# One matmul per group written as two of 128 columns, in a two-block network on one core

## The reference, cut to what matters

```
proj = rmsnorm(h) @ w_in + b_in
h = h + merged @ w_out
h = h + (silu(gate) * val) @ w_down        # gate, val from rmsnorm(h) @ w_up
...
proj = rmsnorm(h) @ w_in_2
h = h + merged @ w_out_2
h = h + square(relu(rmsnorm(h) @ mlp_w1)) @ mlp_w2
```

## Time and profile before

| | |
|---|---|
| median of three runs | 2766.68 us |
| the profiled execution's own time | 2776.59 us |
| its span, first to last instruction | 2774.7 us |
| TensorE busy | 2727.6 us (98%), 22990 matmuls |
| VectorE busy | 1702.0 us (61%) |
| ScalarE busy | 1294.1 us (47%) |
| mean granted TensorE clock | 0.993 of full |
| bytes moved by DMA | 503.31 MB, mean 181 GB/s |

### The profile page before, as it was taken

The page is one execution under the profiler, slowest core; times in us unless marked ns, Lnnn a source line. Parts: engine busy times, 40 slices in busy tenths (PEclk is TensorE's granted clock), DMA queues, the critical chain, the costliest instruction groups (busy, mean ns, idle before and its releaser), DMA issues.

```text
span 2774.7 us, 53033 instructions
## 1 busy us (share of the span) xinstructions
PE 2727.6 (98%) x22990; PEld 2710.7 (98%) x22990; DVE 1702.0 (61%) x1727; ACT 1294.1 (47%) x1458; POOL 1.8 (0%) x14
## 2 busy tenths in 40 slices
PE   7999999999999999999989999999999999999998
PEld 6999999999999999999989999999999999999998
DVE  4555564566667567646785687676665455554555
ACT  4444544444545345434553466664444343343443
POOL 0000000000000000000000000000000000000000
PEclk9999999999999999999999999999999999999999
DMA  5446555555555555555545555555555555555652
GB/s 190 142 148 197 193 186 184 190 187 183 181 188 190 189 194 188 193 191 171 171 149 182 169 181 182 183 197 193 189 189 189 182 182 195 183 184 187 191 183 107
DMA packets 257822, 503.31 MB, mean 181 GB/s; under 512 B 10150, under 2 KB 19038, under 8 KB 257630
## 3 DMA queue, kind: packets, MB, share of 16 engines
q1 hardware_dynamic: 255348, 500.50, 54.7%
q10 hardware_dynamic: 2298, 0.26, 0.1%
HBM read 498.63 MB, written 2.10 MB: 180 GB/s over the span
## 4 chain that ended last, share of the span: by engine, by line
PE 93%; DVE 4%; ACT 2%; issue 1%; ACTq 0%; DVEq 0%
PE psum L547 28%; PE psum L548 28%; PE psum L549 28%; PE psum L574 2%; PE psum L575 2%; PE psum L576 2%; DVE wlo L1289 1%; ACT whi L864 1%; DVE work L1317 0%; DVE hn L1327 0%; ACT hn L885 0%; DVE work L1614 0%; ACTq L853 0%; PE psum L787 0%; PE psum L789 0%
## 5 line engine op out<-in xcount | busy, mean ns | idle before, releaser
L1289 DVE TENSOR_TENSOR wlo<-raw,whi 128x1024 fp32r<-128x1024 f32 x952 | 1160.3, 1223 | 977.0 <-ACT whi L864 974.8
L864 ACT ACTIVATE whi<-raw 128x1024 fp32r<-128x1024 f32 x952 | 1003.6, 1058 | 1299.1 <-PE psum L549 1186.6
L547 PE MATMUL psum<-hn,whi 128*128 128x256 f32 x4448 | 1248.9, 281 | 10.8 <-DVE wlo L1289 10.6
L548 PE MATMUL psum<-hn,whi 128*128 128x256 f32 x4448 | 1246.0, 280 | 0.0
L549 PE MATMUL psum<-hn,wlo 128*128 128x256 f32 x4448 | 1245.9, 280 | 0.0
L547 PEld LDWEIGHTS psum<-hn,whi 128*128 128x128 f32 x4448 | 845.9, 190 | 15.1 <-issue 12.9
L549 PEld LDWEIGHTS psum<-hn,wlo 128*128 128x128 f32 x4448 | 842.9, 190 | 0.0
L548 PEld LDWEIGHTS psum<-hn,whi 128*128 128x128 f32 x4448 | 841.2, 189 | 0.1
L547 PE MATMUL psum<-act,whi 128*128 128x256 f32 x2544 | 714.1, 281 | 13.8 <-DVE wlo L1289 9.7
L549 PE MATMUL psum<-act,wlo 128*128 128x256 f32 x2544 | 713.5, 280 | 0.0
L548 PE MATMUL psum<-act,whi 128*128 128x256 f32 x2544 | 713.4, 280 | 0.0
(11 more groups left out here) (220 smaller groups left out, 949.9 us busy)
## 6 DMA issues: line engine op xcount, KB each, us to landing
raw<-in_w_in SPq DMA_DIRECT2D x160, 1024.0 KB, 5.1
raw<-in_mlp_w SPq DMA_DIRECT2D x128, 1024.0 KB, 5.2
raw<-in_w_up SPq DMA_DIRECT2D x80, 1024.0 KB, 5.0
raw<-in_w_down SPq DMA_DIRECT2D x40, 1024.0 KB, 5.1
raw<-in_w_out SPq DMA_DIRECT2D x32, 1024.0 KB, 5.1
raw<-in_w_branch_m SPq DMA_DIRECT2D x8, 1024.0 KB, 5.0
raw<-in_w_branch_c SPq DMA_DIRECT2D x8, 1024.0 KB, 5.1
raw<-in_w_up SPq DMA_DIRECT2D x8, 768.0 KB, 4.4
```

Of the source, the lines that this page charges most:

```text
L547: mm(o, hi[:, kk, w], both[:, 0, :], start=first and m % 2 == 0, stop=False)
L548: mm(o, hi[:, kk, w], both[:, 1, :], start=False, stop=False)
L864: A(whi[:, n % SLOTS, :], raw[:, n // 2 % RAW, n % 2 * HALF:(n % 2 + 1) * HALF], ACT.Copy)\
L1289: V.tensor_tensor(wlo[:, n % SLOTS, :], raw[:, n // 2 % RAW, n % 2 * HALF:(n % 2 + 1) * HALF], whi[:, n % SLOTS, :].bitcast(F32), ALU.subt ...
```

## The change

In the second half of every group, for the first row tile and the first output tile, the product of the high weights with the high activations is issued as two matmuls with the same weights, one over token columns 0 to 127 and one over 128 to 255. Neither has a start flag; the old one had none there either. The rest of the program is as it was.

```diff
                         for m in range(tiles):
                             o = psum[:, 4 * s + m // 2, m % 2 * T:(m % 2 + 1) * T]
                             w = slice(m * P, (m + 1) * P)
-                            mm(o, hi[:, kk, w], both[:, 0, :], start=first and m % 2 == 0, stop=False)
+                            if k == 1 and kk == 0 and m == 0:
+
+                                mm(o[:, 0:P], hi[:, kk, w], both[:, 0, 0:P], start=False, stop=False)
+                                mm(o[:, P:T], hi[:, kk, w], both[:, 0, P:T], start=False, stop=False)
+                            else:
+                                mm(o, hi[:, kk, w], both[:, 0, :], start=first and m % 2 == 0, stop=False)
                             mm(o, hi[:, kk, w], both[:, 1, :], start=False, stop=False)
```

## The result

The changed kernel takes **2730.07 us**, the median of four runs (2727.45 to 2732.62), against 2766.28 us for the kernel before. The ratio is 0.9862, with a 95% interval of 0.9816 to 0.9907. It is 36 us faster, where 12.8 us slower was forecast. The profiled execution's own time went from 2776.59 to 2727.69 us.

A forecast was written before the change was run, and what follows sets the result against it. TensorE, busy 98% of the span, was taken to bound the kernel. Of 118 pairs, five were given away: (118 - 4 - 1) x 0.1133 = +12.8 us on 2766.68 gives 2779.5 us, range 2774.5 to 2792.

The forecast's parts named there:

- the unit of everything below: Pace of 256-column float32r matmuls on TensorE, read from 1999.93 to 2003.67 us: 0.1133 us each, used to price every pair.
- The other groups keep 0.1133 us: Expected sign in the changed profile: matmuls outside the pairs go on stepping at 0.1133 us.
- 118 pairs: Count of groups going through `group`, each getting one pair, so TensorE should have 118 matmuls more.
- +0.113 us a pair, bound by the weight load: Each narrow matmul takes 0.113 us for its weight load, so a pair costs 0.226 against 0.113.
- The single distances of 0.113 us: Expected sign in a steady stretch: narrow matmul, second narrow one and following wide one start 0.113 us apart each.
- No less than nothing: Low end kept for a pair's cost: 0, if only moving columns counted; high end +0.327 us, or +0.414.
- `down_2` keeps its length: TensorE idled 13.1 us in 64 us there, so its four pairs were put at nothing; 0.45 us if uncovered.
- The cheap pair: Rival: narrow weight loads are fast or overlapped, so +0 to +2.9 us in all, 2766.7 to 2769.6; chance 0.09.
- the switch: Rival: the narrow pair also costs one step of 0.087 us, 23.6 us in all, about 2790; chance 0.05.
- the full-precision pace: Rival: a 128-column float32r matmul takes 0.22 us, 38.6 to 48.9 us in all, 2805 to 2816; chance 0.10.
- The 16-column transposes' 0.069 us: Step read for the 16-column transposes, 1.10 / 16, taken as evidence of a faster kind of weight load.
- The Trainium skill's rule: Page's sustained 81 ns per 128-column matmul with load: +49 ns a pair, +5.8 us in all; isolated formula +0.3 us.

## Why the prediction was wrong

The step that failed is in the first part: "33 steps, 3.74 / 33 = 0.1133 us each", and "That is the unit of everything below". It was true of 4 us at 2000 us and was carried to the whole program, down to the last part, where "The other groups keep 0.1133 us". Two thirds of the matmuls ran at 117.8 ns, and no rival had a place for it.

By the steps of the forecast:

- *118 pairs*: right.
- *+0.113 us a pair, bound by the weight load*: right. 352 more pairs cost 0.113 us each, and the loads start 0.11 us apart across a pair.
- *The single distances of 0.113 us*: wrong in form. They are 0.06, 0.11 and 0.17, three times 0.113 in sum. The second narrow matmul starts 0.06 us behind the start of its own load (707.31 and 707.25), where the others stand 0.11 behind theirs.
- *No less than nothing*: wrong, and not by a mis-sized term but by a missing one. The sum with it: (13989 - 543) long matmuls fewer, 4.5 ns each, is -60.5 us; the pairs are 118 x 0.127 = +15.0 us; together -45.5 us. The profiled execution lost 48.9 us. The other 3 us I did not trace. Laid side by side by instruction, 1200 matmuls took 4.6 us less where the kernel before was in the long rhythm (from 2180 us on), and 0.5 to 1.0 us more where both were in the short one (887 to 1160 us): the pairs alone.
- *`down_2` keeps its length*: right. The 64 us of the earlier trace rows took 63.8 us before and 63.6 us after, from the start of one instruction to that of the same other.
- *The cheap pair, the switch, the full-precision pace*: none took place. A step like the switch's does stand behind each pair (0.17), but it is part of the 0.127. The switch's price of 0.087 us was misread to begin with: in the earlier trace rows the first float32r matmul is followed late, after 0.20 us, but it also starts early, 0.14 us behind the two records that otherwise take 0.22. Together that is 0.34 us, and 0.22 + 0.12 without a seam: nearly nothing.
- *The 16-column transposes' 0.069 us*: it has the last one's latency in it. Their starts are 0.062 us apart; no term of the sum hangs on it.
- *The Trainium skill's rule*, "TensorE: Matmul & The Clock Gate", section "Back-to-back issue gap", with 81 ns for 128 columns and their loads: the runs speak against it for narrow float32r matmuls that stand between wide ones, at 0.113 us for a further pair in place of a wide matmul, so 113 ns for each narrow one; a sustained stream of 128-column float32r matmuls, which is what the page speaks of, no run has. The estimate by that page's formula for the isolated matmul, +0.3 us in all, fits still less.

Why -36 us in the medians and -49 in the profiles: the kernel before was profiled in one of its longer executions. In the experiments its runs went from 2750.56 to 2791.81 us, the changed kernel's from 2727.45 to 2732.62. A width of 40 us is 9000 matmuls at 4.5 ns. That the runs differ by how many matmuls fall into the long rhythm would fit, but it is not shown: the other runs have no trace, and the kernel with one pair had 16134 long ones in its profiled run and was only 4 us slower than the kernel before in its own, where 2145 more of them would make 9.7 us. The forecast's scatter of 2.5 us came from three runs; 31 later runs of the kernel before lie between 2750.56 and 2782.05 us.

**The warning was in the rows.** 20976 matmuls of 256 columns at my unit are 2377 us, 1728 of 272 at 0.126 are 218, and the 286 others at 0.215 at most are 61: 2656 us. The page has 2727.6 us busy. Of the 72 us missing, the long rhythm is 13989 x 4.5 ns = 63 us. Most of the rest is some 120 matmuls at 0.213 us, 0.1 us more each, while the granted clock was at its lower level, 1.2 GHz (so the clock's mean from 1368 to 1376 us, behind a wait in `down_2`, is 0.79). Two windows of TensorE (900 to 1140 us with 2120 matmuls, 2100 to 2700 with 5097) would have told.

**What stays open** is what the two rhythms are. The traces show that a TensorE stall can change them: at 356 us the kernel before goes from short to long, at 895 from long to short. The full-precision sums of squares in `up_0` and `mlp1_0` left the long one each time, 26 of 26 in the thirteen traces. The granted clock was 1.00 in both, and in both each load starts 2 to 5 ns behind the matmul ahead. Why one or three narrow matmuls mostly flip and two reset, why eight single ones in a row did not flip, and why the cut at 192 or the halves apart reset in half of the cases only, I don't know.

## What to carry to other kernels

A unit price from a few microseconds of trace must be multiplied up and laid beside the engine's busy time; a gap of a few per cent can be a second pace, as here, and on the bounding engine that outweighs what a small change costs. Look for it with the number of instructions per microsecond in several windows. Where the stream of wide float32r matmuls has two paces, as here, one matmul cut in two in the middle, now and then, costs 0.13 us and puts it into the shorter; directly behind full-precision matmuls that is not sure.

## What the runs showed of the hardware that was not expected

- With 256-column float32r matmuls, each with its load, TensorE keeps 113.3 ns or 117.8 ns a matmul for thousands of matmuls without a break (6046 at 117.8 ns in the kernel before, from 2047 to 2759 us; 2300 at 113.3 ns there, from 896 to 1156 us), at a granted clock of 1.00.
- One narrow matmul (128 columns) or three mostly flip between the two (106 of 114 and 105 of 109 places). Two of 128 columns side by side ended the longer one in 32 of 32 cases; cut at 192 and 64 it was 5 of 10, with two wide ones between the halves 8 of 18, and four pairs in a row 8 of 10.
- At 272 columns there was one pace, 126 ns, with and without pairs.
- A narrow matmul's successor can start 58 ns after it, but the loads keep 0.11 us, and the next one gives the time back.
